# The first head's banded keys loaded early, and other slots for maxima and output batches, in a hybrid attention and mixture-of-experts layer

## What is computed

```python
proj = rmsnorm(x) @ w_in            # queries, keys, values of three head groups
# A: 8 heads, each with three branches: compressed blocks (C), all earlier keys (X), a band of 512 keys (Y)
s = q @ k.T * scale - slope * dist  # per branch; softmax, times V; o = sum of gate * branch
# F: 4 heads with a forget bias; D: 4 heads, each the difference of two softmax maps
x = x + concat(o_A, o_F, o_D) @ w_out
x = x + moe(rmsnorm(x))             # 32 experts, two per token
return rmsnorm(x)
```

## Time and profile before

| | before |
|---|---|
| runs, us | 1373.25, 1369.82, 1365.38; median 1369.82 |
| the profiled execution, us | 1367.83, of it the span 1365.9 |
| mean granted clock of TensorE | 0.924 |
| PE busy | 1194.6 us (87%) |
| VectorE (DVE) busy | 626.0 us (46%) |
| ScalarE (ACT) busy | 399.1 us (29%) |
| GpSimd (POOL) busy | 199.1 us (15%) |
| DMA | 261.60 MB, mean 192 GB/s |

### The profile page before, as it was taken

The page is one execution under the profiler, slowest core; times in us unless marked ns, Lnnn a source line. Parts: engine busy times, 40 slices in busy tenths (PEclk is TensorE's granted clock), DMA queues, the critical chain, the costliest instruction groups (busy, mean ns, idle before and its releaser), DMA issues.

```text
span 1365.9 us, 22552 instructions
## 1 busy us (share of the span) xinstructions
PE 1194.6 (87%) x8298; PEld 866.5 (63%) x8298; DVE 626.0 (46%) x1567; ACT 399.1 (29%) x716; POOL 199.1 (15%) x447
## 2 busy tenths in 40 slices
PE   1899899996998999999989899929999999999840
PEld 1889788775776878888767688724444444444310
DVE  3330344233564676665675423363343434343327
ACT  5221112221353555444765222201111111111102
POOL 3020000001211111211542100010000000000024
PEclk8899999998797999999998999959999999999975
DMA  7010744355256445544534333173999999999527
GB/s 300 32 47 32 253 154 139 139 169 139 64 118 209 102 113 127 121 102 110 166 108 141 140 112 101 68 332 128 367 369 366 366 369 375 361 367 371 201 100 285
DMA packets 71484, 261.60 MB, mean 192 GB/s; under 512 B 20929, under 2 KB 29409, under 8 KB 61793
## 3 DMA queue, kind: packets, MB, share of 16 engines
q1 hardware_dynamic: 59584, 217.37, 48.2%
q0 software_dynamic: 7056, 25.69, 5.0%
q10 hardware_dynamic: 4752, 17.30, 3.1%
HBM read 206.71 MB, written 53.48 MB: 190 GB/s over the span
## 4 chain that ended last, share of the span: by engine, by line
PE 77%; DVE 9%; DMA 6%; issue 3%; SPq 2%; POOL 2%; ACT 1%; ACTq 0%; POOLq 0%; DVEq 0%
PE PS L1943 16%; PE PS L1671 11%; PE PS L1818 9%; PE PS L1958 8%; PE PS L1883 7%; PE PS L1660 5%; PE PS L1762 4%; PE PS L1798 4%; PE PS L1799 3%; PE PS L1935 2%; DMA k<-T_d 2%; PE PS L1792 2%; DMA q<-shr 1%; POOL y L838 1%; DMA wst<-in_wt 1%
## 5 line engine op out<-in xcount | busy, mean ns | idle before, releaser
L1943 PE MATMUL PS<-wgu,XT 128*128 128x512 f32 x512 | 227.9, 598 | 4.0 <-DVE XT L1554 3.1
L997 ACT ACTIVATE pt<-PS,cst 128x512 f32<-128x512 f32 (+3 forms) x288 | 172.3, 650 | 173.6 <-PE PS L1799 139.6
L1303 DVE CUSTOM_DVE_ANT_0 junkm<-PS,cst 128x512 f32<-128x512 f32 (+3 forms) x276 | 136.9, 532 | 101.9 <-PE PS L1762 99.0
L1943 PEld LDWEIGHTS PS<-wgu,XT 128*128 128x128 f32 x512 | 98.1, 192 | 127.9 <-issue 125.6
L1818 PE MATMUL PS<-V,pt 128*64 128x65 f32 x3840 | 160.2, 236 | 0.0
L1818 PEld LDWEIGHTS PS<-V,pt 128*64 128x64 f32 x3840 | 136.2, 147 | 35.2 <-issue 23.2
L1958 PE MATMUL PS<-wdn,aT 128*128 128x512 f32 x256 | 115.4, 593 | 1.9 <-ACT aT L850 1.9
L1762 PE MATMUL PS<-k,q 128*128 128x128 f32 (+3 forms) x336 | 95.6, 363 | 20.3 <-DMA k<-T_d 13.3
L771 POOL TENSOR_SCALAR_AFFINE_SELECT pt<-pt 128x128 f32<-128x128 f32 x224 | 67.6, 305 | 273.6 <-ACT pt L997 225.8
L1671 PE MATMUL PS<-hTh,wth 128*128 128x512 f32 x256 | 102.6, 401 | 4.5 <-DVE wtl L1153 4.5
L1559 DVE TENSOR_SCALAR ge<-PS 128x256 f32<-128x256 f32 x32 | 13.6, 425 | 200.3 <-PE PS L1943 200.3
(11 more groups left out here) (272 smaller groups left out, 1774.9 us busy)
## 6 DMA issues: line engine op xcount, KB each, us to landing
wgu<-in_wgu SPq DMA_DIRECT2D x33, 2048.0 KB, 11.0
wdn<-in_wdn SPq DMA_DIRECT2D x33, 1024.0 KB, 13.1
Y_d<-YO ACTq DMA_DIRECT2D x33, 512.0 KB, 2.6
q<-T_d SPq DMA_DIRECT2D x60, 256.0 KB, 4.9
k<-T_d SPq DMA_DIRECT2D x60, 256.0 KB, 5.6
wst<-in_wt SPq DMA_DIRECT2D x16, 512.0 KB, 6.4
T_d<-thi SPq DMA_DIRECT2D x16, 512.0 KB, 2.6
T_d<-tlo SPq DMA_DIRECT2D x16, 512.0 KB, 3.9
```

Source lines behind the costliest of these rows:

```text
L997: ins = nc.scalar.activation(pt[:, (n + 2) % 6, 0:nt * P], PS[:, n % 4, 0:nt * P], ACT.Exp, scale=C("slopes", h, h + 1), bias=C("kb", w, w ...
L1303: V_.tensor_tensor_reduce(out=junk_[:, n % 2, 0:L], in0=PS[:, bank, 0:L], in1=tab, scale=1.0, scalar=-3e38, op0=ALU.add, op1=ALU.max, accu ...
L1943: ins = mm(PS[:, 2 + p, :], XT[:, p, c, :], wgu[q][:, c, :], start=(c == 0), stop=(c == KC - 1))
```

## The change

```diff
-    LEAD, DEEP = 9, 2
+    LEAD, DEEP = {"X": 10, "Y": 10, "C": 5, "F": 9, "D": 9}, 2
...
-                    at_ = 1 + k // 3 if n == 2 else slot - self.LEAD + k // 2
+                    at_ = k // 3 if n == 2 else slot - self.LEAD[x.kind] + k // 2
...
-                    self.out_at.setdefault(slot + k // 2 + self.DEEP + 1, []).append((x, c))
+                    late = x.kind == "C" and c == 0
+                    self.out_at.setdefault(slot + k // 2 + self.DEEP + 1 + late, []).append((x, c))
...
-        junka, junkm = (at(n, [P, 2, 512], f32, o) for n, o in (("junka", ZD + 32 * KB), ("junkm", ZB + 48 * KB)))
+        junka, junkm = at("junka", [P, 512], f32, ZD + 32 * KB), at("junkm", [P, 2, 512], f32, ZB + 48 * KB)
+        K1y = at("K1y", [P, SEQ], f32r, ZD + 34 * KB)
...
                 for dst, half, part, r0 in ((Q1, 0, 0, q0), (Q1, 1, 1, q0), (K1, 0, 0, k0), (K1, 1, 0, k0),
-                                            (Q2, 0, 0, q0), (K2, 0, 1, k0)):
+                                            (Q2, 0, 0, q0), (K2, 0, 1, k0))[4 * (x.n == 2):]:
...
             load_unit(PLAN.full[0])
+            sp_.wait_ge(act_did, AC.of("c1v"))
+            sp_.wait_ge(pe_did, PEV.of("ov"))
+            sp_.wait_ge(t_st[1], 32 * 5 + 1)
+            for half in range(2):
+                sp_.dma_start(K1y[HD * half:HD * half + HD, :].bitcast(f32), T_r[0, G_KW * P:G_KW * P + HD, :])\
+                   .then_inc(ky_in, 16)
             pair_of_groups(6)
...
                 if f:
                     shift_row(x)
-                if f and x.kind == "X":
-                    shift_row(PLAN.units[x.n + 1])
...
                     stored += 1
+                if f and x.kind == "X":
+                    shift_row(PLAN.units[x.n + 1])
...
                 dve.wait_ge(m_ready, n + 1)
-                if n >= 2:
+                if x.n < 2 and n:
+                    dve.wait_ge(mx_done, n)
+                elif n >= 2:
                     dve.wait_ge(mx_done, n - 1)
...
+            def operands(x):
+                q1, k1 = (Q1[3], K1y) if x.n == 2 else (Q1[x.set], K1[x.set])
+                return q1, Q2[x.set], k1, K2[x.set]
...
-                if k == 0 and x.kind != "C":
-                    pe_.wait_ge(ld_in[s], 96 * ((PLAN.full.index(x) - 1) // 3 + 1 if x.n else 1))
+                if k == 0 and x.n == 2:
+                    pe_.wait_ge(ky_in, 32)
+                elif k == 0 and x.kind != "C":
+                    pe_.wait_ge(ld_in[s], loaded(x))
```

More of the change, by code:

```diff
@@ L270, in program @@
                           for k, n in enumerate(("q1_", "q2_", "k1_", "k2_")))
-        junka, junkm = (at(n, [P, 2, 512], f32, o) for n, o in (("junka", ZD + 32 * KB), ("junkm", ZB + 48 * KB)))
+        junka, junkm = at("junka", [P, 512], f32, ZD + 32 * KB), at("junkm", [P, 2, 512], f32, ZB + 48 * KB)
+        K1y = at("K1y", [P, SEQ], f32r, ZD + 34 * KB)
         oh = at("oh", [P, 2, NT, HD], f32, ZB + 52 * KB)
         tmp = at("tmp", [P, NT, HD], f32, ZB + 56 * KB)
-        shra, shr = (at(n, [8, 3, P], f32r, o) for n, o in (("shra", ZD + 36 * KB), ("shr", ZB + 58 * KB)))
+        shra, shr = at("shra", [8, 2, P], f32r, ZD + 38 * KB), at("shr", [8, 3, P], f32r, ZB + 58 * KB)
         identr, trimr = (at(n, [P, P], f32r, ZB + 60 * KB + 512 * k) for k, n in enumerate(("identr", "trimr")))
@@ L393, in program @@
         z_in = sem("z_in")
+        ky_in = sem("ky_in")
         ld_in = [sem(f"ld_in{u}") for u in range(4)]
@@ L634, in _ @@
                     stored += 1
+                if f and x.kind == "X":
+                    shift_row(PLAN.units[x.n + 1])
+                if f and PLAN.full[f - 1].kind in "YF":
                     if stored == NSA_H + FOX_H:
@@ L1282, in maxima @@
                 n, b = x.m_use[k], x.n % 3
-                junk_ = junka if x.n < 2 else junkm
+                junk_ = junka[:] if x.n < 2 else junkm[:, n % 2, :]
                 bank = M_BANK[n % 2]
                 dve.wait_ge(m_ready, n + 1)
-                if n >= 2:
+                if x.n < 2 and n:
+                    dve.wait_ge(mx_done, n)
+                elif n >= 2:
                     dve.wait_ge(mx_done, n - 1)
                 if x.kind == "C":
-                    chain(V_.tensor_tensor(out=junk_[:, n % 2, :], in0=PS[:, bank, :], in1=C("distc"), op=ALU.add))
-                    V_.tensor_reduce(out=mx[:, b, 0, :], in_=junk_[:, n % 2, :].rearrange("p (t c) -> p t c", t=NT),
+                    chain(V_.tensor_tensor(out=junk_, in0=PS[:, bank, :], in1=C("distc"), op=ALU.add))
+                    V_.tensor_reduce(out=mx[:, b, 0, :], in_=junk_.rearrange("p (t c) -> p t c", t=NT),
                                      axis=AX.X, op=ALU.max).then_inc(mx_done, 1)
@@ L1302, in maxima @@
                     tab = C("dist", off, off + L)
-                V_.tensor_tensor_reduce(out=junk_[:, n % 2, 0:L], in0=PS[:, bank, 0:L], in1=tab, scale=1.0,
+                V_.tensor_tensor_reduce(out=junk_[:, 0:L], in0=PS[:, bank, 0:L], in1=tab, scale=1.0,
                                         scalar=-3e38, op0=ALU.add, op1=ALU.max,
@@ L1744, in _, with loaded @@
             spread(5, 6)
+            def loaded(x):
+                f = PLAN.full.index(x)
+                return 96 * ((f - 1) // 3 + 1) - 64 * (x.set == 0) if f else 96
+            def operands(x):
+                q1, k1 = (Q1[3], K1y) if x.n == 2 else (Q1[x.set], K1[x.set])
+                return q1, Q2[x.set], k1, K2[x.set]
             def max_pass(x, k):
                 n, s = x.m_use[k], x.set
+                q1, q2, k1, k2 = operands(x)
                 bank = M_BANK[n % 2]
-                if k == 0 and x.kind != "C":
-                    pe_.wait_ge(ld_in[s], 96 * ((PLAN.full.index(x) - 1) // 3 + 1 if x.n else 1))
+                if k == 0 and x.n == 2:
+                    pe_.wait_ge(ky_in, 32)
+                elif k == 0 and x.kind != "C":
+                    pe_.wait_ge(ld_in[s], loaded(x))
                 if n >= 2:
@@ L1754, in max_pass @@
                     for t in range(NT):
-                        ins = mm(PS[:, bank, t * HD:(t + 1) * HD], Q1[s][:, t * P:(t + 1) * P],
+                        ins = mm(PS[:, bank, t * HD:(t + 1) * HD], q1[:, t * P:(t + 1) * P],
                                  kc1[:, x.g * HD:(x.g + 1) * HD], start=True, stop=True)
@@ L1759, in max_pass @@
                 t, c, k0, nk = x.m[k]
-                q_, k_ = (Q2[s][0:96], K2[s][0:96]) if x.kind == "D" else (Q1[s][:], K1[s][:])
+                q_, k_ = (q2[0:96], k2[0:96]) if x.kind == "D" else (q1[:], k1[:])
                 edge = x.kind == "F" and k0 + nk == t + 1
@@ L1780, in scores @@
                     pe_.wait_ge(aug_set[s], 2)
+                    if x.n == 2:
+                        pe_.wait_ge(ld_in[s], loaded(x))
                 if k == 0 and x.kind == "C":
@@ L1791, in scores @@
                 if x.kind == "D":
-                    ins = mm(o, K2[s][0:97, j * P:(j + 1) * P], Q2[s][0:97, q], start=True, stop=True)
+                    ins = mm(o, k2[0:97, j * P:(j + 1) * P], q2[0:97, q], start=True, stop=True)
                 elif x.kind == "C":
                     mm(o, identr[:], maskc[:, q], start=True, stop=False)
-                    mm(o, kc1[:, HD * x.g:HD * x.g + P], Q1[s][:, q], start=False, stop=False)
-                    ins = mm(o, kc2[0:97, HD * x.g:HD * x.g + P], Q2[s][0:97, q], start=False, stop=True)
-                else:
-                    mm(o, K1[s][:, j * P:(j + 1) * P], Q1[s][:, q], start=True, stop=False)
-                    ins = mm(o, K2[s][0:HD + 1, j * P:(j + 1) * P], Q2[s][0:HD + 1, q], start=False, stop=True)
+                    mm(o, kc1[:, HD * x.g:HD * x.g + P], q1[:, q], start=False, stop=False)
+                    ins = mm(o, kc2[0:97, HD * x.g:HD * x.g + P], q2[0:97, q], start=False, stop=True)
+                else:
+                    mm(o, k1[:, j * P:(j + 1) * P], q1[:, q], start=True, stop=False)
+                    ins = mm(o, k2[0:HD + 1, j * P:(j + 1) * P], q2[0:HD + 1, q], start=False, stop=True)
                 ins.then_inc(s_ready, 1)
```

## The result

| | before | after |
|---|---|---|
| median of six runs, us | 1365.17 (1363.98 to 1373.25) | 1379.67 (1374.91 to 1388.97) |
| ratio after/before | | 1.0099, 95% interval 1.0059 to 1.0140 |
| the profiled execution, us | 1367.83, span 1365.9 | 1388.97, span 1387.0 |
| mean granted clock of TensorE | 0.924 | 0.920 |

A forecast was written before the change was run, and what follows sets the result against it. PE's work, waits and clock were taken to set attention's length. Terms -5.5 + 0 + 10.3 + 5.0 + 1.5 + 3.7 = +15.0 us on 1367.83 gave 1383 us, range 1366 to 1392.

The forecast's parts named there:

- Step 1: Y0's maxima in slots 0 to 3: the first wait moves to X1's first maximum, about 7 us; -5.5 us.
- I take 19 us: Length assumed for the slow stretch behind the first wait, between 21.3 and 16.5 us.
- Step 2: K1y's load, two fewer loads and junka: PE's work on groups 12 and 13 covers the delayed weights; 0 us.
- Step 3: C's maximum beside Y's passes: PE waits 1.27 us for DVE in seven heads, +8.9 us.
- The 1.4 us for late row copies: Second pass of the slot after C's, waiting for C's row copy: 0.2 us in seven heads, +1.4 us.
- Step 4: Before Y's first pass: waits for keys of 2.1 us instead of 1.17 in five heads; together +5.0 us.
- The formula by which the keys would have been in time: Trainium skill's DMA cost, 2.0 us plus bytes at 436 GB/s: Y's keys in time, sum 4 us less.
- Step 5: Y2's row behind the 4 MB output weights: PE waits 8.3 us instead of 6.8, +1.5 us.
- Step 6: TensorE's clock in attention: seven to eight falls at twelve places, 2.5 more at 1.5 us, +3.7 us.
- every wait makes a fall: Rival: the clock falls 12 times instead of 7.5 at attention's waits, 1390 us; chance 0.17.
- the forecast's own case: Whole kernel about 1383 us, reaching from 1377 to 1389, with seven to eight clock falls; chance 0.50.
- The rival on the other side: C's maximum has DVE to itself and keys are early, so waits and five falls go: 1349 us; chance 0.10.

The follow-up runs named there:

- e1: The kernel before with only the early load of K1y with Y0 in slots 0 to 3, all leads 9: 1356.01 us, ratio 0.9919 to before.
- e9: The kernel before with the early keys of Y0, leads of 9 for X, Y and C, and C's second batch a slot later: 1345.86 us, ratio 0.9844.
- e6: The changed kernel with X and Y 9 slots ahead instead of 10, C's lead still 5: 1364.21 us, ratio 0.9984 to before.
- e12: e9 with the output weights issued as one MB in each of four rounds: 1334.87 us, ratio 0.9774 to before.
- e2: The changed kernel with C's lead 10 instead of 5, so C's maximum stands alone in its slot: 1382.90 us, ratio 1.0111 to before.
- e13: e9 with the four loads that the maxima need counted on a semaphore apart from the scores' two: 1349.82 us, ratio 0.9873 to before.
- e3: The changed kernel with maxima waiting only for their own four loads, the scores' two counted apart: 1371.34 us, ratio 1.0026 to before.
- e4: The changed kernel with the output weights in four parts of 1 MB, one in each of four rounds: 1373.39 us, ratio 1.0053 to before.
- e5: The kernel before with leads of 10, 10 and 5, C's late batch and C's row moved, without K1y's early load: 1388.20 us, ratio 1.0170.
- e7: e9 with both the output weights in four pieces and the maxima's loads counted apart: 1336.24 us, ratio 0.9778 to before.
- e8: The changed kernel with C's lead 10 and the maxima's loads counted apart, both at once: 1364.25 us, ratio 0.9980 to before.

## Why the prediction was right, point by point

The forecast was 1383 us, the median is 1379.67. Its direction and size hold, but two steps were off by some 5 and 12 us, with opposite signs, in the profiled execution, by which I take the steps as they were made.

**Step 1 (start), -5.5 forecast, -10.3 measured.** The wait came where it was placed: 5.97 us at 340.92, with the keys landing at the forecast 341.0. The term that failed is "I take 19 us" for the slow stretch behind it; it was 5.5 us. I had priced it by the length of the wait before it, and that does not set it (last section). With 5.5 us the step's own formula gives -12.2, so some 2 us of the shadowed work did not come as sized. e1 shows the gain by itself: 0.8%, some 11 us. **Step 2 (K1y's load, junka), 0:** nothing contradicts it; attention starts at 325.54 before and at 325.37 after.

**Step 3 (behind C), +8.9 forecast, 8.3 measured:** seven waits of 1.19 instead of 1.27 us. The 1.4 us for late row copies did not come separately; the one wait for a copy is 0.9 us, in head 1.

**Step 4 (batches and Y's load), +5.0 forecast.** Five waits for keys of 1.2 to 1.9 us, 7.1 together (the one at 578.53 is labelled POOL, but that pass waits for no work of GpSimd, and it starts 9.4 us after its load was asked for at 569.11, as in the other heads), 0.9 in head 1, six of 0.58 us at the values, less the 7.0 us removed: +4.5. The size holds, the make-up only in part: the wait at the output bank stood in no step. The formula by which the keys would have been in time, weighed in that step, does not hold for these loads, which SP issues: asked for at 500.33, Y5's keys let PE go on at 509.81, 9.5 us later.

**Step 5 (row behind the weights), +1.5 forecast:** 8.58 instead of 6.8 us, +1.8, and the slow stretch there is 17.1 instead of 20.5 us.

**Step 6 (clock), +3.7 forecast, about 15 measured in the profiled execution.** This is the step that failed. The price was too low by its own rows: 30.86 - 29.14 is 1.72 us for a fall, not 1.5. I took seven or eight of twelve places; ten of the twelve had a stretch at 0.50, an eleventh stood at head 1's row copy, and three were twice as long as I had priced, for a reason I don't know. In units of 3.4 us that is 14 instead of 5, nine more at 1.7 us. The rival "every wait makes a fall" came nearer on the clock, the forecast's own case on the waits. Even that rival's upper end, +10.5, was below what the profiled execution shows. For the median run the estimate above, some 7 us, leaves a miss of only 3.

**The sum:** -10.3 + 8.3 + 4.5 + 1.8 - 1.7 + 15.3 = 17.9 us: -10.3 at the start and 28.2 in the seven heads, just what the stretches above show; the other 2.3 of attention's 20.2 us come in the F and D heads, where I had forecast nothing. Of these, 1.3 us are longer waits for rows in the D heads (1.7 us at L1792 before, 3.0 at L1818 after); what made those rows later is open. The two errors partly cancel: 5 us too little gained at the start, 12 too little lost by the clock. Step by step the forecast of +15.0 stands against +21.1 between the profiled executions. That the medians, 14.5 us apart, come so near to it is luck in part: by the estimate above, the clock's part between the median runs is some 8 us less than between the profiled ones.

**The rival on the other side,** that C's late batch frees DVE, was right in one half: e9 shows that this edit gains. In the change the gain was lost: C moved at once beside Y's passes, where it waits for DVE anyway (e6).

By the ratios the parts of the change are: keys -0.8% (e1), late batch -0.75% (e9), C beside Y with its row +1.4% (e6), leads of 10 +1.2% (after), each some 0.5% to either side. They add up to +1.0% by the way they are formed, each from the one before.

## What to carry to other kernels

Price a wait on TensorE with the clock behind it: here the new waits of the heads, 14.6 us, cost 15.3 us more by the falls of the clock in the profiled execution (an estimated 7 in the median run), and shortening a wait from 1.17 to 0.81 us gained 0.75% while it saved 2.4 us of waiting. Compare the clocks of all runs, too, before a trace of one is taken for all. A change made of several moves is best taken apart by runs: two of these four moves were gains, and e12 keeps them. And before a wait is removed, look at which transfer it covers (e2, e13): the next one in the queue takes its place, and one has to take away both.

## What the runs showed of the hardware

**The length of a wait does not set the slow stretch behind it.** After the first wait PE ran at 0.50 for 21.3 us where the wait was 10.7 (before), for 5.5 us where it was 6.0 (after); but for some 19 us after a wait of 3.4 us for Y0's row (e13, 349.06 to 368.5), and 12.7 us after the row's 8.6 (after). I found no rule for it; the runs don't separate what PE did before from what it did behind the wait.

**Short waits of about 1.2 us often had falls behind them, those of up to 0.8 us had none.** At C's maximum or two passes behind it, the waits of 1.16 to 1.20 us have a stretch at 0.50 that begins within 2.5 us of their end in 5 of 6 cases before, 5 of 7 in after, 4 of 6 in e1, 5 of 7 in e3, 4 of 7 in e4, 3 of 7 in e5 and 3 of 7 in e6: 29 of 47. The waits there of 0.54 to 0.81 us have none in e9, e12, e7 and e13, 24 waits in all. So a wait of 1.2 us makes a fall likely and not certain; what decides is not shown. In e8, with 0.56 and 1.58 us close together, falls stand at C's place in every head. The Trainium skill ("TensorE: Matmul & The Clock Gate", section "Loop structure matters more than you think") has it that a VectorE copy between groups of matmuls doesn't break TensorE's warmth, where the next matmuls follow immediately. e12, with waits of 0.81 us, agrees; before, after and e1, where PE waits 1.17 to 1.19 us for VectorE, do not.

**Small rows pay for what is ahead of them on their queue.** A 4 KB row behind 4 MB of weights kept PE waiting 5.5 to 9.0 us in the kernels that had it so; with the weights in parts of 1 MB (e4, e7, e12) it didn't wait there at all.
